# Last adaLN product moved from the attention steps to the output tiles, convolution projections spread over 22 steps

## The chip, the core and the metric

The kernel runs on one core of one Trainium2 chip. The metric is the device time of one execution in microseconds (us). TensorE (PE) does the matmuls, VectorE (DVE), ScalarE (ACT) and GpSimd (POOL) the rest, and SyncE (SP) issues most of the transfers. Each engine goes through its own list of instructions in order and waits on semaphores for the others.

## What is computed

One inference step of one decoder layer, for 512 prompt rows and 8 samples with a cache of 4096 rows each, all in float32. Cut to what matters here:

```python
sh1, sc1, ga1, sh2, sc2, ga2 = _adaln(c, w_ada, b_ada, 6)
h = _rms_norm(x, g_norm1) * (1.0 + sc1) + sh1
q, k, v, logf, conv_in, gate_b = _mixer_inputs(h, w_in, b_forget)   # gate_c * u, gate_b
attn = attend(q, k, v, logf)          # prompt: 512 rows; samples: 8 x 4096 cached rows
conv_y, new_buf = _short_conv(conv_in, conv_buf, conv_w)
x = x + ga1 * _merge_heads(attn, conv_y, gate_b, g_attn_out, g_conv_out, w_out)
h = _rms_norm(x, g_norm2) * (1.0 + sc2) + sh2
x = x + ga2 * _hier_moe(h, ...)       # 32 experts, 2 of them per row
...
shp, scp = _adaln(c_prompt, w_ada_final, b_ada_final, 2)
y_prompt = _rms_norm(xp, g_final) * (1.0 + scp) + shp
```

`_adaln(c, w, b, n)` is `silu(c) @ w + b`, cut into n parts. The product with `w_ada_final` (1024 x 2048, 8 MB) is used only at the very end, in the last norm. "The last adaLN product" is that one.

## The kernel before, in words

The order of all work is written out by hand, engine by engine. It has these parts:

- **Setup and projections** (to 187 us): the first adaLN product, the norm, and the projections for q, k and v. Every projection of the input is a "section" of 512 columns, loaded in two halves ("units" of 1 MB, u = 2 * section + half) into the three slots of region R_w. A slot is loaded again when its unit has been used.
- **The loop of 32 steps** (187 to 434 us), `for w in range(NT * H)`: step w is one head of one block of 128 prompt rows. On TensorE a step transposes the probabilities (`turn`, L644), in odd steps makes the scores of the next two heads (`score_pair`, L628 and L633), does some blocks of the convolution's three sections (`conv_block`, which calls L547; sections 3, 4 and 5 have 8 blocks each, and the table `CONV_IN_STEP` says which step does which), then one or two chunks of the samples' values (`values`, L512), then probabilities times v (`weigh`, L654). On VectorE a step takes one chunk of the samples' keys (`k_chunk`, L1503 and L1505), in odd steps the row maxima of the next two heads (`row_max`, L1671 and L1674), and the convolution's gates and taps. So `turn(w + 1)` can't begin before VectorE has passed `row_max(w + 1)`, which stands behind the key chunk of an odd step w.
- **The cache stream**: 64 key chunks and 64 value chunks of 1 MB each, alternating, gathered by GpSimd (L2121) into a ring of five slots in region R_kv. A chunk is asked for when the chunk five places before it has been used, and GpSimd waits for that in order.
- **The last adaLN product**, `late_ada(k)`, k = 0 to 7: 1 MB of `w_ada_final` and four matmuls (L385; each is two passes in the trace) into bank 1, in steps 19 to 26. SyncE loads the eight units (`late_load`, L2252) into the same three slots of R_w as units 12 to 19.
- **Output tiles** (from 434 us): `out_tile(t, after)` is eight parts of two matmuls with w_out (L802); behind the parts named in `after` stands one value chunk. Around them stand second norms, router (`route`, L877), and for the rest of the cache stream 11 key chunks and 22 value chunks.
- **Experts** (from 606 us): 32 experts with 3 MB of weights each, in five slots. Slot 0 is region R_q, where the loop has q, k and v.

SyncE's transfers go in order too: after the conv sections it issues the last adaLN units, some small vectors, w_out (into R_w once the last adaLN units have been used), and then, when the loop is over, the experts.

Of the kernel before, what the change touches and what calls it, by code (L numbers as in the profile page):

```python
# [44 lines left out]
SECS = 512  # L45


def build(nc, x_prompt, x_sample, c_prompt, c_sample, cache_k, cache_v, cache_logf, state_conv,
# [6 lines left out]
    with ctx:  # L55
# [81 lines left out]
        w_unit = view(R_w, 0, [3, 4, SECS])  # L137
        x_a = view(R_x, 0, [5, D])
# [183 lines left out]
        def step_values(w):  # L322
# [3 lines left out]
        CONV_IN_STEP = {0: (3, (0, 1)), 1: (3, (2,)), 2: (3, (3, 4)), 3: (3, (5,)), 4: (3, (6, 7)),  # L326
                        5: (4, (0,)), 6: (4, (1, 2)), 7: (4, (3,)), 8: (4, (4,)), 9: (4, (5,)), 10: (4, (6, 7)),
                        11: (5, (0,)), 12: (5, (1,)), 13: (5, (2,)), 14: (5, (3,)), 15: (5, (4,)), 16: (5, (5,)),
                        17: (5, (6,)), 18: (5, (7,))}
        SQUARE_AT = {14: 0, 16: 1, 18: 2, 20: 3, 21: 4}  # L330
# [44 lines left out]
        def _(pe):  # L375
# [365 lines left out]
            def spread_chunk(j):  # L741

                if j == 0:
                    pe.wait_ge(b_loaded[0], 32)
                out = take(0, ("mod_spread", j + 1) if j < 4 else ("mod_scaled", j - 3))
                spread_wide(j, out[:, :]).then_inc(S["expand_done"], 1)
# [11 lines left out]
            for w in range(NT * H):  # L758
# [48 lines left out]
            def out_tile(t, after):  # L807
                for half in range(2):
                    for k0 in range(0, KD, 2):
                        out_part(t, half, k0)  # L810
                        if 4 * half + k0 // 2 in after:
                            values(1)

            def sample_sums():

                pe.wait_ge(S["sum_ready"], B)
                for c in range(C4):
# [46 lines left out]
            def route(i):  # L864
# [4 lines left out]
                if i == 0:  # L869
                    pe.wait_ge(S["wr_loaded"], 64)  # L870
                    pe.wait_ge(S["part_ready"], 4)
# [179 lines left out]
        def _(act):  # L1051
# [52 lines left out]
            def ada_evac(g):  # L1104
                act.wait_ge(S["ada_done"], g + 1)
                copy(part[:, g - 1, :], bank[5 if g < 3 else 1][:, :]).then_inc(S["part_ready"], 1)
# [93 lines left out]
            def spread_evac(j):  # L1200
                act.wait_ge(S["expand_done"], j + 1)
                half = slice((j % 2) * SECS, (j % 2 + 1) * SECS)
                copy((ga1_p if j < 2 else sh2_p)[:, half], bank[0][:, :]).then_inc(S["mod_spread"], 1)
# [40 lines left out]
            for w in range(NT * H):  # L1244
# [22 lines left out]
                if w == 19:  # L1267
# [11 lines left out]
                if w == LAST_ADA_AT[-1] + 1:  # L1279
                    ada_evac(3)  # L1280
# [57 lines left out]
            sample_exp(7)  # L1338
            rows_turned(1)
# [90 lines left out]
        def _(dve):  # L1430
# [267 lines left out]
            def spread_scale(j):  # L1698
# [5 lines left out]
                V.scalar_tensor_tensor(sc2_p[:, lo], bank[0][:, :], 1.0, sc2_p[:, lo], ALU.add, ALU.mult)\  # L1704
# [10 lines left out]
            for w in range(NT * H):  # L1715
                if w in (7, 8, 10, 11):
                    gate_in({7: 0, 8: 1, 10: 2, 11: 3}[w])
                if w in (13, 15, 17, 19):
                    gate_out((w - 13) // 2)
                if w == 11:  # L1720
                    sample_gate_in()
                if w == 19:
                    sample_gate_out()
                if w in (27, 28):
                    spread_scale(w - 23)
# [9 lines left out]
                if 9 <= w < 13:  # L1735
                    taps(w - 9)
                if w == 12:
# [491 lines left out]
        def _(sp):  # L2229
# [17 lines left out]
            def late_load(k):  # L2247

                u = 12 + k
                name, count = unit_free["w", u - 3]  # L2250
                sp.wait_ge(S[name], count)
                sp.dma_start(w_unit[:, u % 3].rearrange("p j c -> p (j c)"), w_fin_v[:, k, :]).then_inc(unit_loaded[u % 3], 16)  # L2252
# [64 lines left out]
            for i in (2, 0, 1):  # L2317
                name, count = unit_free["w", 17 + (i + 1) % 3]
                sp.wait_ge(S[name], count)
                sp.dma_start(view(R_w, i * 2048, [2, D]), w_out_v[:, 2 * i:2 * i + 2, :]).then_inc(S["wo_loaded"], 16)  # L2320
            sp.wait_ge(S["part_ready"], 4)
            sp.dma_start(bias_rows(2), row(b_ada_final).rearrange("o (j c) -> (o j) c", c=SECS)).then_inc(b_loaded[1], 16)
# [21 lines left out]
            sp.wait_ge(S["outs"], 16 * 8)  # L2344
            sp.wait_ge(S["k_used"], NKV)
# [80 lines left out]
```

## Time and profile before

| | |
|---|---|
| median of three runs | 905.0 us (903.67 to 905.01) |
| profiled execution, its device time | 904.93 us |
| its span, first to last instruction | 903.1 us |
| TensorE busy | 754.0 us (83%) |
| VectorE busy | 532.7 us (59%) |
| moved by DMA | 311.80 MB, mean 345 GB/s |

The profiled execution is 0.07 us from the median, so sums can be made against it; 1.8 us of it lie outside the span. All times below count from the start of the span. No engine is busy throughout: the page gives shares over stages that have different limits, so each stage is read by itself.

### The profile page before, as it was taken

The page shows a single profiled execution, that of the slowest core. Times are in us where ns is not written, and L with a number is a line of the kernel's source. Part 1 is how long each engine was busy: PE and PEld are TensorE (multiplying, and loading weights), DVE is VectorE, ACT ScalarE, POOL GpSimd, SP SyncE. Part 2 cuts the span into 40 slices and gives each one's busy share as a digit, 9 for nine tenths or more (in the row PEclk, how much of TensorE's full clock was granted, in tenths as well). Part 3 has the DMA queues.
Part 4 walks back from the last instruction along what each step waited for, and adds up shares of the span by engine and source line. Part 5 has one row for each costly group of instructions (what it writes and reads, how often), then busy time and mean ns, then how long its engine had stood idle before and what let it go on. Part 6 is the DMA issues. An engine that isn't in the chain of part 4 may idle for free.

```text
span 903.1 us, 9755 instructions
## 1 busy us (share of the span) xinstructions
PE 754.0 (83%) x3872; PEld 356.9 (40%) x3872; DVE 532.7 (59%) x659; ACT 171.3 (19%) x359; POOL 269.6 (30%) x271
## 2 busy tenths in 40 slices
PE   4979999789999999889877797849999877878720
PEld 1623333234444333334322334425555544545500
DVE  3196896878499997598988812561333222222238
ACT  3200211021131233222301210322111101111102
POOL 2462124434235352523364310012232222222100
PEclk9889999999999995955899798758999999999965
DMA  8999599998997999999799984655999999999643
GB/s 346 397 409 407 208 347 364 416 418 335 353 327 293 374 379 419 408 362 419 307 365 369 375 338 186 256 196 195 411 408 411 410 409 411 410 409 406 254 154 148
DMA packets 67140, 311.80 MB, mean 345 GB/s; under 512 B 12195, under 2 KB 12687, under 8 KB 42006
## 3 DMA queue, kind: packets, MB, share of 16 engines
q1 hardware_dynamic: 39994, 161.11, 45.3%
q0 software_dynamic: 24496, 145.65, 41.0%
q10 hardware_dynamic: 2604, 4.40, 1.3%
q8 instruction: 31, 0.51, 0.2%
q14 instruction: 15, 0.12, 0.0%
HBM read 304.42 MB, written 14.98 MB: 354 GB/s over the span
## 4 chain that ended last, share of the span: by engine, by line
PE 38%; DMA 26%; DVE 20%; SPq 6%; issue 5%; ACT 2%; POOL 1%; POOLq 0%; DVEq 0%; ACTq 0%
PE bank L547 7%; DMA R_kv<-in_cache_k_dram,kv_index 6%; DVE R_kv L1503 6%; PE bank L965 6%; DMA R_kv<-in_w_expert_up_dram 5%; DVE R_sc L1505 4%; PE bank L512 4%; PE bank L989 3%; PE bank L802 3%; DMA R_w<-in_w_expert_up_dram 3%; DMA R_q<-in_w_expert_up_dram 3%; DMA R_cm<-in_w_expert_up_dram 3%; DMA R_kv<-in_cache_v_dram,kv_index 3%; DMA R_cm<-in_w_ada_dram 2%; SPq L2334 2%
## 5 line engine op out<-in xcount | busy, mean ns | idle before, releaser
L2121 POOL DMA_INDIRECT R_kv<-in_cache_k_dram,kv_index x64 | 99.0, 1546 | 164.6 <-DVE R_sc L1505 102.0
L1505 DVE TENSOR_REDUCE R_sc<-R_kv 128x32 f32<-128x2048 f32 x64 | 146.3, 2286 | 2.2
L547 PE MATMUL bank<-R_h,R_w 128*128 128x512 f32 x320 | 145.4, 604 | 0.0
L1503 DVE TENSOR_TENSOR R_kv<-R_kv,R_m 128x2048 f32<-128x2048 f32 x56 | 128.1, 2288 | 25.5 <-DMA R_kv<-in_cache_k_dram,kv_index 25.2
L2121 POOL DMA_INDIRECT R_kv<-in_cache_v_dram,kv_index x64 | 73.6, 1150 | 145.3 <-DVE R_sc L1505 79.6
L512 PE MATMUL bank<-R_kv,R_sc 128*8 128x512 f32 x512 | 76.1, 683 | 27.8 <-DMA R_kv<-in_cache_v_dram,kv_index 27.8
L547 PEld LDWEIGHTS bank<-R_h,R_w 128*128 128x128 f32 x320 | 59.4, 192 | 76.7 <-issue 75.6
L2183 POOL DMA_INDIRECT expert_rows_scratch<-R_h,R_m x32 | 32.2, 1007 | 188.9 <-DVE R_h L1979 188.9
L1970 DVE COPY R_h<-bank 128x128 f32<-128x128 f32 x32 | 9.3, 292 | 103.1 <-PE bank L981 103.1
L1974 DVE SCALAR_TENSOR_TENSOR R_h<-bank,R_m 128x512 f32<-128x512 f32 x32 | 24.0, 751 | 73.6 <-PE bank L989 73.6
L967 PE MATMUL bank<-R_kv,R_h 128*64 128x256 f32 x208 | 50.8, 401 | 0.0
L802 PE MATMUL bank<-R_w,R_cm 128*128 128x512 f32 x96 | 46.7, 626 | 1.0 <-issue 1.0
L1391 ACT ACTIVATE R_h<-bank 64x256 f32<-64x256 f32 x32 | 12.1, 377 | 186.3 <-PE bank L967 186.3
L2179 POOL DMA_INDIRECT R_t<-h_scratch,R_m x32 | 32.9, 1030 | 41.6 <-DVE R_m L1888 32.1
L512 PEld LDWEIGHTS bank<-R_kv,R_sc 128*8 128x8 f32 x512 | 8.9, 89 | 77.6 <-issue 38.8
L654 PEld LDWEIGHTS bank<-R_q,R_t 128*128 128x128 f32 x160 | 24.3, 224 | 33.4 <-issue 33.4
L1061 ACT ACTIVATE R_h<-bank 128x512 f32<-128x512 f32 (+1 forms) x41 | 24.5, 597 | 61.0 <-PE bank L974 46.6
L965 PE MATMUL bank<-R_kv,R_h 128*64 128x256 f32 x112 | 27.1, 398 | 7.1 <-DMA R_kv<-in_w_expert_up_dram 6.4
L965 PE MATMUL bank<-R_q,R_h 128*64 128x256 f32 x112 | 28.1, 408 | 5.5 <-DMA R_q<-in_w_expert_up_dram 4.7
L547 PE MATMUL bank<-R_w,R_h 128*128 128x512 f32 x64 | 30.9, 627 | 0.0
L965 PE MATMUL bank<-R_sc,R_h 128*64 128x256 f32 x96 | 23.5, 401 | 8.6 <-DMA R_kv<-in_w_expert_up_dram 8.6
L1061 ACT ACTIVATE R_t<-bank 128x512 f32<-128x512 f32 (+6 forms) x36 | 15.0, 420 | 79.4 <-PE bank L644 77.2
(371 smaller groups left out, 1225.3 us busy)
## 6 DMA issues: line engine op xcount, KB each, us to landing
R_cm<-in_w_ada_dram SPq DMA_DIRECT2D x19, 1024.0 KB, 9.3
R_kv<-in_w_expert_up_dram SPq DMA_DIRECT2D x13, 1024.0 KB, 23.2
R_kv<-in_w_expert_down_dram SPq DMA_DIRECT2D x13, 1024.0 KB, 22.4
R_w<-in_w_in_dram SPq DMA_DIRECT2D x12, 1024.0 KB, 11.8
R_w<-in_w_ada_final_dram SPq DMA_DIRECT2D x8, 1024.0 KB, 9.7
R_q<-in_w_expert_gate_dram SPq DMA_DIRECT2D x7, 1024.0 KB, 16.6
R_q<-in_w_expert_up_dram SPq DMA_DIRECT2D x7, 1024.0 KB, 22.7
R_q<-in_w_expert_down_dram SPq DMA_DIRECT2D x7, 1024.0 KB, 22.1
```

Of the source, the lines that this page charges most:

```text
L512: last = nc.tensor.matmul(out[32 * j:32 * j + H, :], scores[:, b, c * CH + j, :], kv_ring[ring_slot[g]][:, j, :], start=(c == 0), stop=(c ...
L547: last = nc.tensor.matmul(out, l, r, start=(k == 0), stop=(k == KD - 1))
L802: last = nc.tensor.matmul(bank[4 + 2 * (t % 2) + half][:, :], m, wo[k][:, half * 512:(half + 1) * 512], start=(k == 0), stop=(k == KD - 1))
L965: nc.tensor.matmul(bank[2 + xs][0:SLOTS, 0:DE], xe_t[xs][:, c, a, :], gw[:, a, c, :], start=(k == 0), stop=(k == 7))
L967: last = nc.tensor.matmul(bank[2 + xs][SLOTS:2 * SLOTS, 0:DE], xe_t[xs][:, c, a, :], uw[:, a, c, :], start=(k == 0), stop=(k == 7))
L989: last = nc.tensor.matmul(bank[4 + xs][half * SLOTS:(half + 1) * SLOTS, :], hid_t[xs][:, k, :], dw[:, k, half * 512:(half + 1) * 512], sta ...
L1061: return nc.scalar.activation(out, in_, ACT.Copy, scale=scale)
L1503: V.tensor_tensor(keys[:, :, :], keys[:, :, :], spread(q, [P, CH, HW]), ALU.mult).then_inc(S["k_products"], 1)
L1505: V.reduce_sum(scores[:, b, s * CH:(s + 1) * CH, :], keys.rearrange("p r (h d) -> p r h d", h=H), AX.X)\
L2121: pool.indirect_dma_start(kv_flat[ring_slot[g]][:, :], None, k_rows if kind == "k" else v_rows, bass.IndirectOffsetOnAxis(kv_index[:, n:n ...
L2179: return pool.indirect_dma_start(x_e[s][:, :], None, h2_dram, bass.IndirectOffsetOnAxis(col, 0), bounds_check=2 * (T + B) - 1, oob_is_err= ...
L2183: return pool.indirect_dma_start(y_dram, bass.IndirectOffsetOnAxis(col, 0), y_e[s][:, :], None, bounds_check=4 * (T + B) - 1, oob_is_err=F ...
```

## The change

The eight `late_ada` calls leave steps 19 to 26. Five stand now among the parts of the first two output tiles, one behind each named part, and three behind the value chunks and router that follow. Their weights go to the three slots of region R_q (`fin_unit`), which is free when the loop is over; SyncE issues them there, ahead of the experts, and expert 0 waits until the product is done. The product uses bank 0 instead of bank 1, and the spreading of the other adaLN parts bank 1 instead of bank 0. The 24 convolution blocks are spread over steps 0 to 21, nearly always one per step (before: 0 to 18, in six steps two or more), and everything behind them (gates, squares, spreads) moves three steps or so later.

```diff
+        fin_unit = view(R_q, 0, [3, 4, SECS])
...
-        CONV_IN_STEP = {0: (3, (0, 1)), 1: (3, (2,)), 2: (3, (3, 4)), 3: (3, (5,)), 4: (3, (6, 7)),
...
+        CONV_IN_STEP = {0: (3, (0, 1)), 1: (3, (2,)), 2: (3, (3,)), 3: (3, (4,)), 4: (3, (5,)), 5: (3, (6,)), 6: (3, (7,)),
...
-        SPREAD_AT = {20: 0, 21: 1, 22: 2, 23: 3, 26: 4, 27: 5}
-        LAST_ADA_AT = range(19, 27)
+        SPREAD_AT = {23: 0, 24: 1, 25: 2, 26: 3, 27: 4, 28: 5}
...
             def late_ada(k):
                 if k == 0:
-                    take(1, ("part_ready", 4))
+                    take(0, ("part_ready", 4))
                 u = 12 + k
                 pe.wait_ge(unit_loaded[u % 3], 16 * w_turn(u))
-                last = ada_block(w_unit[:, u % 3], k, bank[1])
+                last = ada_block(fin_unit[:, u % 3], k, bank[0])
...
-                if w == 19:
+                if w == 22:
                     conv_rows()
-                if w in LAST_ADA_AT:
-                    late_ada(w - LAST_ADA_AT[0])
...
-            out_tile(0, (1, 3, 5, 7))
-            out_tile(1, (1, 3, 5, 7))
+            out_tile(0, (1, 3, 5, 7), {4: 0, 6: 1})
+            out_tile(1, (1, 3, 5, 7), {0: 2, 4: 3, 6: 4})
             gather_values(5)
-            values(2)
+            values(1)
+            late_ada(5)
+            values(1)
             turn_rows(0)
+            late_ada(6)
             route(0)
-            values(2)
+            values(1)
+            late_ada(7)
+            values(1)
...
-            for k in range(3):
-                late_load(k)
-
             sp.wait_ge(S["acc_done"], 24)
             sp.wait_ge(S["samp_done"], 6)
-            for k in range(3, 8):
-                late_load(k)
...
             sp.wait_ge(S["pv_done"], NT * H)
             sp.wait_ge(S["outs"], 16 * 8)
+            for k in range(8):
+                late_load(k)
+            sp.wait_ge(S["part_ready"], 4)
+            sp.dma_start(bias_rows(2), row(b_ada_final).rearrange("o (j c) -> (o j) c", c=SECS)).then_inc(b_loaded[1], 16)
+            sp.wait_ge(S["ada_done"], 4)
             sp.wait_ge(S["k_used"], NKV)
             gate_up(0, 0)
```

How this moves instructions shows best in the order on TensorE. First step 2 of the loop (L644 is the turn at its head, L547 the convolution, four matmuls to a block, L512 a value chunk, L654 the weighing):

```order
 L654 MATMUL bank<-R_q,R_t 128x64
 L644 MATMUL bank<-ident,R_t 128x128
-L547 MATMUL bank<-R_h,R_w 128x512 x8
+L547 MATMUL bank<-R_h,R_w 128x512 x4
 L512 MATMUL bank<-R_kv,R_sc 8x512 x4
 L654 MATMUL bank<-R_q,R_t 128x64
```

One of the step's two blocks has gone to step 3; steps 4, 6 and 10 lose one in the same way, and three blocks of section 5 go beyond step 18. Then TensorE at steps 20 to 22, where the three blocks arrive (L385 is one unit of the last adaLN product, L732 a spread, L678 the samples' columns of the section just done):

```order
-L385 MATMUL bank<-R_w,c_t 32x512 x4
-L732 MATMUL bank<-R_p,selp 128x512
+L547 MATMUL bank<-R_h,R_w 128x512 x4
 L512 MATMUL bank<-R_kv,R_sc 8x512 x4
 L654 MATMUL bank<-R_q,R_t 128x64 x3
...
-L385 MATMUL bank<-R_w,c_t 32x512 x4
-L732 MATMUL bank<-R_p,selp 128x512
+L547 MATMUL bank<-R_h,R_w 128x512 x4
+L678 MATMUL bank<-sel,R_m 128x8 x4
 L512 MATMUL bank<-R_kv,R_sc 8x512 x4
```

A unit of the product and a spread have gone from each step, and a block of the convolution has come. Third, the second half of the first output tile in the change (L800 is the line of the output matmuls there, L385 now reads R_q):

```order
L800 MATMUL bank<-R_w,R_cm 128x512 x2
L385 MATMUL bank<-R_q,c_t 32x512 x4
L800 MATMUL bank<-R_w,R_cm 128x512 x2
L512 MATMUL bank<-R_kv,R_sc 8x512 x4
L800 MATMUL bank<-R_w,R_cm 128x512 x2
L385 MATMUL bank<-R_q,c_t 32x512 x4
L800 MATMUL bank<-R_cm 128x512 x2
L512 MATMUL bank<-R_kv,R_sc 8x512 x4
```

Before, the same place has only the output matmuls (L802) and the value chunks:

```order
L802 MATMUL bank<-R_w,R_cm 128x512 x4
L512 MATMUL bank<-R_kv,R_sc 8x512 x4
L802 MATMUL bank<-R_w,R_cm 128x512 x2
L802 MATMUL bank<-R_cm 128x512 x2
L512 MATMUL bank<-R_kv,R_sc 8x512 x4
```

So two value chunks have a unit of the product ahead of them there, and each unit waits for its own megabyte.

## Rows read from the trace of the kernel before

**Rows 1.** Stretches: PE, PEld, DVE, ACT, POOL busy us (x instructions), granted clock, DMA share, GB/s.

```profile
199.07:246.62 47.55, 47.36 (x205) 20.09 (x204) 31.85 (x30) 7.68 (x26) 16.41 (x14) 1.00 0.93 359
187.00:332.50 145.50, 142.70 (x631) 60.66 (x632) 122.34 (x134) 32.69 (x89) 58.70 (x57) 0.99 0.91 349
332.00:362.00 30.00, 27.05 (x119) 10.82 (x120) 22.79 (x22) 7.79 (x22) 7.85 (x7) 0.64 1.01 419
332.50:434.00 101.50, 92.26 (x432) 37.52 (x431) 81.03 (x76) 27.62 (x64) 34.47 (x29) 0.70 1.01 404
361.70:434.00 72.30, 66.01 (x320) 27.49 (x319) 58.53 (x55) 19.83 (x42) 26.92 (x22) 0.72 1.01 397
434.00:457.00 23.00, 17.46 (x77) 5.59 (x76) 20.85 (x24) 7.17 (x13) 8.13 (x8) 0.84 0.71 270
457.00:507.00 50.00, 36.79 (x140) 13.73 (x138) 42.12 (x29) 4.92 (x9) 25.52 (x19) 0.87 0.98 388
507.00:606.00 99.00, 79.80 (x393) 39.77 (x392) 46.26 (x125) 23.33 (x46) 7.95 (x16) 0.80 0.66 255
606.00:847.00 241.00, 209.04 (x1450) 126.84 (x1452) 64.71 (x117) 31.12 (x62) 62.10 (x61) 0.96 0.97 386
```

**Rows 2.** TensorE in order of time: step 2 and the head of step 3.

```profile
204.99 0.28 PE L644 MATMUL bank<-ident,R_t 128*128 128x128 f32 x1
205.11 7.03 PE L547 MATMUL bank<-R_h,R_w 128*128 128x512 f32 x16
213.32 0.28 PE L644 MATMUL bank<-ident,R_t 128*128 128x128 f32 x1
```

**Rows 3.** VectorE in order of time, step 7; in brackets idle before, and its releaser.

```profile
242.05 0.69 DVE L1607 TENSOR_TENSOR R_cm<-bank,R_cm 128x512 f32<-128x512 f32 x1 [6.86 <-PE bank L547]
```

**Rows 4.** TensorE: heads of steps 19, 20, 22, and instructions of steps 19 and 21.

```profile
332.54 0.50 PE L644 MATMUL bank<-ident,R_t 128*128 128x128 f32 x3
335.19 1.07 PE L385 MATMUL bank<-R_w,c_t 128*32 128x512 f32 x8
337.89 1.04 PE L512 MATMUL bank<-R_kv,R_sc 128*8 128x512 f32 x8 [1.63 <-DMA R_kv<-in_cache_v_dram,kv_index]
342.86 0.87 PE L644 MATMUL bank<-ident,R_t 128*128 128x128 f32 x3 [1.32 <-ACT R_cm L1061]
354.63 1.94 PE L385 MATMUL bank<-R_w,c_t 128*32 128x512 f32 x8
356.50 2.07 PE L732 MATMUL bank<-R_p,selp 32*128 32x512 f32 x2
361.66 0.85 PE L644 MATMUL bank<-ident,R_t 128*128 128x128 f32 x3
```

**Rows 5.** VectorE in order of time: the key chunk of step 25.

```profile
383.39 2.29 DVE L1503 TENSOR_TENSOR R_kv<-R_kv,R_m 128x2048 f32<-128x2048 f32 x1 [4.18 <-DMA R_kv<-in_cache_k_dram,kv_index]
```

**Rows 6.** SyncE: issues of the product's units 1 to 2 and 6 to 7; their landing.

```profile
323.75 6.74 SPq L2252 DMA_DIRECT2D R_w<-in_w_ada_final_dram  x2
364.43 6.62 SPq L2252 DMA_DIRECT2D R_w<-in_w_ada_final_dram  x2
DMA to landing us min/median/max: 8.7/9.7/9.9
```

**Rows 7.** The chain that ended last, first half of the loop: start, us, what.

```profile
222.99 7.64 DMA R_w<-in_w_in_dram
```

**Rows 8.** Groups by line, 434 to 507 us: busy, mean ns | idle before, releaser.

```profile
L1503 DVE TENSOR_TENSOR R_kv<-R_kv,R_m 128x2048 f32<-128x2048 f32 x11 | 25.2, 2289 | 7.4 <-DMA R_kv<-in_cache_k_dram,kv_index 7.3
L512 PE MATMUL bank<-R_kv,R_sc 128*8 128x512 f32 x96 | 15.5, 725 | 16.6 <-DMA R_kv<-in_cache_v_dram,kv_index 16.6
```

**Rows 9.** The chain that ended last, behind the second output tile.

```profile
490.90 9.89 DMA R_kv<-in_cache_v_dram,kv_index
502.73 1.82 PE bank L861 x8
505.71 1.98 PE bank L877 x16
```

More of the change, by code:

```diff
@@ L744, in spread_chunk @@
                     pe.wait_ge(b_loaded[0], 32)
-                out = take(0, ("mod_spread", j + 1) if j < 4 else ("mod_scaled", j - 3))
+                out = take(1, ("mod_spread", j + 1) if j < 4 else ("mod_scaled", j - 3))
                 spread_wide(j, out[:, :]).then_inc(S["expand_done"], 1)
@@ L805, in out_part, with out_tile @@
                     last.then_inc(S["wo_done"], 1)
-            def out_tile(t, after):
+            def out_tile(t, after, ada={}):
                 for half in range(2):
@@ L810, in out_tile @@
                         out_part(t, half, k0)
-                        if 4 * half + k0 // 2 in after:
+                        part_no = 4 * half + k0 // 2
+                        if part_no in after:
                             values(1)
+                        if part_no in ada:
+                            late_ada(ada[part_no])
             def sample_sums():
                 pe.wait_ge(S["sum_ready"], B)
+                pe.wait_ge(S["part_ready"], 4)
                 for c in range(C4):
@@ L1105, in ada_evac @@
                 act.wait_ge(S["ada_done"], g + 1)
-                copy(part[:, g - 1, :], bank[5 if g < 3 else 1][:, :]).then_inc(S["part_ready"], 1)
+                copy(part[:, g - 1, :], bank[5 if g < 3 else 0][:, :]).then_inc(S["part_ready"], 1)
             def sample_exp(b):
@@ L1202, in spread_evac @@
                 half = slice((j % 2) * SECS, (j % 2 + 1) * SECS)
-                copy((ga1_p if j < 2 else sh2_p)[:, half], bank[0][:, :]).then_inc(S["mod_spread"], 1)
+                copy((ga1_p if j < 2 else sh2_p)[:, half], bank[1][:, :]).then_inc(S["mod_spread"], 1)
             def spread_samples(half, done):
@@ L1338, in _ @@
             sample_exp(7)
+            ada_evac(3)
             rows_turned(1)
@@ L1703, in spread_scale @@
                 lo = slice((j % 2) * SECS, (j % 2 + 1) * SECS)
-                V.scalar_tensor_tensor(sc2_p[:, lo], bank[0][:, :], 1.0, sc2_p[:, lo], ALU.add, ALU.mult)\
+                V.scalar_tensor_tensor(sc2_p[:, lo], bank[1][:, :], 1.0, sc2_p[:, lo], ALU.add, ALU.mult)\
                     .then_inc(S["mod_scaled"], 1)
@@ L1715, in _ @@
             for w in range(NT * H):
[L1716 to L1720, printed above, removed]
+                if w in (9, 11, 13, 14):
+                    gate_in({9: 0, 11: 1, 13: 2, 14: 3}[w])
+                if w in (16, 18, 20, 22):
+                    gate_out((w - 16) // 2)
+                if w == 14:
                     sample_gate_in()
-                if w == 19:
+                if w == 22:
                     sample_gate_out()
-                if w in (27, 28):
-                    spread_scale(w - 23)
+                if w in (28, 29):
+                    spread_scale(w - 24)
                 if w in (29, 30, 31):
@@ L2316, in _ @@
                 sp.dma_start(wo[k], w_out_v[:, k, :]).then_inc(S["wo_loaded"], 16)
-            for i in (2, 0, 1):
-                name, count = unit_free["w", 17 + (i + 1) % 3]
+            for i in range(3):
+                name, count = unit_free["w", 9 + i]
                 sp.wait_ge(S[name], count)
                 sp.dma_start(view(R_w, i * 2048, [2, D]), w_out_v[:, 2 * i:2 * i + 2, :]).then_inc(S["wo_loaded"], 16)
-            sp.wait_ge(S["part_ready"], 4)
-            sp.dma_start(bias_rows(2), row(b_ada_final).rearrange("o (j c) -> (o j) c", c=SECS)).then_inc(b_loaded[1], 16)
             wg = w_expert_gate.rearrange("l e (a p c) f -> (l e) p a (c f)", a=2, c=4)
```

26 lines of the change are left out of this document (12 added, 14 removed).

## Prediction

> **What bounds the kernel now.** I read the page's slices first, cut the span into stretches where their pattern changes, and then looked in each stretch for the wait that ends last. Four stretches matter.
>
> Steps 0 to 18 (187 to 332.5 us): TensorE is busy 142.7 of 145.5 us at a clock of 0.99, VectorE only 122.3 [rows 1]. A step with two convolution blocks shows why: its two blocks are 7.03 of the 8.33 us from one turn to the next [rows 2], so a block is 3.5 us. VectorE has about 4.6 us of key chunk per step and then waits for TensorE, up to 6.86 us at a time [rows 3]. TensorE sets the pace, by the crowded steps. DMA moves 349 GB/s, below the 419 it shows at its fullest [rows 1].
>
> Steps 19 to 31 (332.5 to 434 us): here DMA moves 404 GB/s, in the first 30 us 419, and both other engines have gaps: TensorE waits for value chunks [rows 4], VectorE for key chunks, at worst 4.18 us [rows 5]. The product's units are in that stream: after the first one, seven of the eight are issued from 323.75 us to 371 us [rows 6]. TensorE also falls to half its clock (1.2 GHz instead of 2.4): a product takes 1.07 us in step 19 and 1.94 us in step 21, and the stretch's mean clock is 0.70 [rows 1, 4]. What the engine did just before the fall were two waits, 1.63 and 1.32 us [rows 4]. So this stretch is bound by DMA, and partly by a slow TensorE.
>
> Output tiles, 434 to 507 us: TensorE waits 16.6 us for value chunks, VectorE 7.3 us for key chunks [rows 8], and the chain goes through a value chunk that took 9.89 us to come [rows 9]. It is a DMA stretch with one gap: from 434 to 457 us only 270 GB/s, afterwards 388 [rows 1]. In the gap the ring is full and VectorE still finishes the loop.
>
> From 507 us on TensorE works through the remaining tiles (chunks and product have to be there by then); the experts after it take 241 us at 386 GB/s [rows 1], whenever they begin.
>
> **The change, part by part.**
>
> *Steps 0 to 18.* Three blocks leave: 3 x 3.5 = 10.5 us less of TensorE. The blocks that only change steps cost the same wherever they stand, as long as TensorE stays the bound, and it does: 142.7 - 10.5 = 132 us against VectorE's 122, of which two gates go to later steps too. Two waits come in. Section 5's second unit is loaded when block 6 of section 4 is done, which is now in step 13, and the samples' rows of section 5 need it in step 14. Behind it stand one block (3.5), the samples' columns (0.9), a value chunk (1.0), weighing, turn and half of the sample rows, about 7.3 us; a unit of w_in took 7.64 us when it was on the chain [rows 7]. Nothing to 3 us; I take 2, with everything later in the loop queued behind. And steps 1 to 6 become short: before 47.55 us, now three blocks and 2 us of sample rows less, 35 us, with 13 chunks and one unit of 1.05 MB each, 14.7 MB or 420 GB/s, where 359 were moved before [rows 1]. Some of it comes out of the ring's store; nothing to 6 us, I take 1.5. Sum: -10.5 + 2 + 1.5 = **-7**.
>
> *Steps 19 to 21.* Before 361.66 - 332.54 = 29.1 us. Of step 19 (10.3 us) 7 stay without product, turned rows and the wait of 1.63. Steps 20 and 21 (18.8 us) ran at half clock; without two products of 1.94 and two spreads of 2.07 they are 10.8, at full clock half of that [rows 4]: 12.5 us in all. Three blocks (10.5) and the samples' columns (0.9) come in. That is dense work, so I take the full clock: 24 us, **-5**. Nothing would be gained if it stayed at half clock.
>
> *Steps 22 to 31.* Before 72.3 us. VectorE was busy 58.5 us, TensorE 66.0 at mixed clocks, DMA moved 28.7 MB [rows 1]. VectorE gets a gate and the scaling with the spread, 60 us. TensorE loses five products and gets two spreads and the turned rows, some 3 us less. DMA loses some 2.5 MB of the product's units, 26.2 MB, at 404 GB/s 65 us. No engine needs more than 66 us, but they didn't overlap fully before either: 69 us, **-3.3**. The ends are 61 us (VectorE alone) and 80 us (TensorE at half clock through most of it: 62 us of work at a mean of 0.72 is 45 at full and 90 at half clock).
>
> *Output tiles to the first routed rows.* The 8.4 MB come in here. The stream in 73 us was 25.6 MB (23 x 270 and 50 x 388 GB/s); with the product 34.0 MB, which at 404 GB/s, what the loop's full stretch keeps up, are 84.2 us: **+11.2**. The first three units, issued when the loop ends, fall into the gap, which has 23 x (419 - 270) = 3.4 MB of room; the other five take turns with key and value chunks. From below: all the room of the stretch at 419 GB/s is used, 34.0 / 0.419 = 81 us, +8. From above: the chunks get half of the 419 GB/s for as long as the product's units flow, 8.4 MB / 0.21 = 40 us; in these they need 40 x 388 = 15.5 MB and get 8.4, which costs 7.1 MB or 17 us. TensorE's products themselves (six, 1.07 us each) hide in its 16.6 us of waits; with that cover gone they are 6 us.
>
> The row for how such a mixture flows is the first 30 us after step 19, where units of the product and chunks ran together: the sum was 419 GB/s, and units landed in 8.7 to 9.9 us [rows 1, 6], 106 to 120 GB/s for each. The Trainium skill ("DMA: Bandwidth & Descriptors", section "Issuing engines are not separate DMA queues") says that transfers issued by scalar, sync or gpsimd run on the same 16 engines and interleave. By it a load that is moved brings no bandwidth, which speaks against this change; the sum above goes the same way by its rows, and the strict half share is the rival below.
>
> *After that.* One product stands between two value chunks at 507 us, where the chain is on TensorE [rows 9]: **+1.1**. The one before it fits between the transposes and the router, where TensorE waits 1.2 us for ScalarE (504.55 to 505.71) [rows 9]. Expert 0's 3 MB, before issued with the last key chunk, now wait for the product; they have some 90 us, in which DMA moves 255 GB/s [rows 1]. Without that cover they would cost 8 us. The other small loads, gates and bank swaps move with the steps they belong to and are hidden by the same engines.
>
> Sum: -7 - 5 - 3.3 + 11.2 + 1.1 = -3.0. The profiled execution took 904.93 us, next to the median of 905.0, so **901.9 us**.
>
> **The rivals.** 0.2% (1.8 us) is about what a measurement of this kernel can tell from no change.
>
> 1. *Forecast: the loop wins some 15 us, the output tiles give back some 12.* 0.42, between 898 and 904.
> 2. *The tiles hide the loads.* If the loop ends nearer VectorE's bound (61 us for steps 22 to 31, -8 more) or the gap takes more than three units, the sum is 891 to 898. For it: 73 us of output tiles hold 5 MB of room at 419 GB/s. Against: the five later units can't be issued in the gap, since their slots are freed by products that stand in the tiles. 0.13.
> 3. *It cancels:* DMA is the bound from step 19 to 507 us in both, the bytes up to there are the same, and TensorE's gain in the first steps is only an earlier arrival at the same stream. For it: all but 40 us of the 320 us are needed at 419 GB/s (117.4 MB). Against: the short first steps use room that was idle (349 GB/s). 903 to 907, 0.21.
> 4. *Slower: the chunks are held to half* while the product's units flow, +17 instead of +11, and the products, each in front of a value chunk, wait for their own unit; a late value chunk holds its ring slot, GpSimd's queue and so the next key chunk. 907 to 910. It decides when the first routed rows come more than 88 us after the loop's end. For it: five slots only, and 16.6 us of waits already. Against: the 419 GB/s of mixed traffic. 0.17.
> 5. *Slower: half clock* in most of steps 22 to 31, 80 us instead of 69: 913. For it: the convolution, which kept TensorE busy, is not there, and the clock was 0.72 in these steps. Against: they were so before too, with less of a gap in between. 0.07.
>
> The range reaches into 2, 4 and 5: **892 to 911**. Faster by over 0.2%, under 903.2: all of 2 and 0.38 of 1, 0.51. Within: the rest of 1 and 0.19 of 3, 0.23. Slower: 4, 5 and the rest of 3, 0.26.
>
> **What would show it.** Step 19 should begin some 138 us after step 0 (before 145.3, from rows 1 and 4), with no step of over 10 us but 0, 13 and perhaps 19; step 22 some 162 us after it; the loop's end at 231 us (before 247). In steps 19 to 21 the blocks should take 3.5 us each, and VectorE's waits for keys be nearly gone. From the loop's end to the router of the first rows some 84 us instead of 72, at over 400 GB/s, with no hole behind the loop. From there to the end the same time as before within 2 us. The forecast is wrong if the loop shortens by less than 10 us, if a product in the tiles waits for its unit by several us, or if key chunks wait over 15 us in sum in the tiles.

## The result, and the profile after

The changed kernel takes 920.4 us, median of four runs (915.7 to 923.9), against 905.0 for the kernel before: ratio 1.014, interval 1.010 to 1.019. Taken again later, beside 25 runs of the kernel before with a median of 907.6, it took 920.6, ratio 1.014 (1.007 to 1.020). The forecast was 901.9 in a range of 892 to 911, so it was wrong, in sign too. Executions more than 1.5% above the fastest of their kernel are left out of the medians and ratios in this document: 2 of 31 and 1 of 23 of the kernel before, 5 of 10 without the product's loads, 2 of 10 with the table alone, 3 of 12 with three units in the loop. The ratios stand as recorded, with their 95% intervals, and differ a little from the quotients of the two medians. The profiled execution of the changed kernel took 923.87 us, its span is 922.1. Its stretches, in the columns of [rows 1], cut where step 0, 19 and 22 begin, where the loop ends, and at the router of the first rows:

```profile
189.16:341.61 152.45, 139.53 (x599) 57.09 (x600) 121.55 (x131) 31.67 (x85) 59.85 (x57) 0.92 0.84 321
341.61:365.69 24.08, 22.76 (x113) 11.14 (x113) 20.33 (x24) 6.52 (x19) 10.75 (x7) 1.00 0.91 349
365.69:443.24 77.55, 71.25 (x290) 31.09 (x289) 61.60 (x56) 21.46 (x46) 28.04 (x23) 0.63 0.88 333
443.24:524.06 80.82, 61.23 (x259) 18.66 (x257) 62.26 (x52) 12.09 (x22) 32.21 (x26) 0.87 1.01 415
524.06:922.10 398.04, 304.82 (x1952) 174.99 (x1948) 140.09 (x281) 63.40 (x126) 73.02 (x80) 0.89 0.81 318
```

Steps 0 to 18 were to shrink from 145.3 to 138 us and have grown to 152.5. The first row shows that this is no longer TensorE's work: it is busy 139.5 of 152.5 us, at a clock of 0.92 where [rows 1] have 0.99. Steps 19 to 21 came out as forecast (24.1 us at full clock), steps 22 to 31 did not (77.6 us against a forecast of 69, at a clock of 0.63). The output tiles take 80.8 us at 415 GB/s (forecast 84), what follows 398.0 (before 397.4).

Two steps hold the loss of the first stretch. TensorE in order of time, steps 7 and 14:

```profile
236.22 0.28 PE L644 MATMUL bank<-ident,R_t 128*128 128x128 f32 x1
237.69 1.07 PE L464 MATMUL bank<-R_w,R_h 128*32 128x512 f32 x8
241.07 1.93 PE L464 MATMUL bank<-R_w,R_h 128*32 128x512 f32 x8 [2.32 <-DMA R_w<-in_w_in_dram]
242.94 5.85 PE L547 MATMUL bank<-R_h,R_w 128*128 128x512 f32 x8
249.96 0.28 PE L644 MATMUL bank<-ident,R_t 128*128 128x128 f32 x1
...
296.50 0.39 PE L644 MATMUL bank<-ident,R_t 128*128 128x128 f32 x2
296.82 1.07 PE L464 MATMUL bank<-R_w,R_h 128*32 128x512 f32 x8
305.96 1.93 PE L464 MATMUL bank<-R_w,R_h 128*32 128x512 f32 x8 [8.07 <-DMA R_w<-in_w_in_dram]
307.82 5.83 PE L547 MATMUL bank<-R_h,R_w 128*128 128x512 f32 x8
315.06 0.39 PE L644 MATMUL bank<-ident,R_t 128*128 128x128 f32 x2
```

L464 is the samples' rows of a new section, one group of matmuls for each half. In step 7 the second half (unit 9) has to be waited for, in step 14 again (unit 11). The wait is only part of the price: behind it TensorE runs at half clock (granted clock 0.61 from 240.0 to 248.8 us, 0.60 from 305.96 to 313.65). Eight such matmuls take 1.93 instead of 1.07 us, the block behind them 5.85 and 5.83 instead of 3.70. Step 7 takes 13.7 us and step 14 18.6. The chain that ended last goes through both loads (start, us, what):

```profile
227.63 13.40 DMA R_w<-in_w_in_dram
290.91 15.01 DMA R_w<-in_w_in_dram
```

They took 13.4 and 15.0 us. For the second the prediction had reckoned with 7.64 [rows 7]; the first it had not looked at. GpSimd, which asks for the cache chunks, shows why the second took so long:

```profile
275.11 0.94 POOL L2126 DMA_INDIRECT R_kv<-in_cache_k_dram,kv_index  x1 [4.56 <-DVE R_sc L1510]
276.41 5.74 POOL L2156 TENSOR_SCALAR_AFFINE_SELECT later<-later 128x64 f32<-128x64 f32 x8 [0.15 <-POOL later L2153]
282.60 0.94 POOL L2126 DMA_INDIRECT R_kv<-in_cache_v_dram,kv_index  x1 [0.44 <-issue]
283.84 0.94 POOL L2126 DMA_INDIRECT R_kv<-in_cache_k_dram,kv_index  x1 [0.30 <-issue]
285.08 1.96 POOL L2126 DMA_INDIRECT R_kv<-in_cache_v_dram,kv_index  x1 [0.31 <-issue]
287.35 0.94 POOL L2126 DMA_INDIRECT R_kv<-in_cache_k_dram,kv_index  x1 [0.30 <-issue]
288.82 0.94 POOL L2126 DMA_INDIRECT R_kv<-in_cache_v_dram,kv_index  x1 [0.54 <-DVE R_sc L1510]
```

Behind key chunk 34 GpSimd builds a small table (`halves`, the 64-column selects). For 5.74 us it asks for nothing, and nothing is left in flight (4 and 0 GB/s from 280 to 284 us). Then it asks for five chunks in 6.2 us. Unit 11 is issued 2 us after the last of them. From its issue to its landing, 290.91 to 305.92 us, the DMA queues moved (packets, MB, share of the 16 engines; q0 holds GpSimd's gathers, q1 SyncE's loads):

```profile
q0 software_dynamic: 681, 4.94, 80.2%
q1 hardware_dynamic: 528, 1.05, 18.3%
```

So the unit shared 400 GB/s with 4.94 MB of chunks: the 2.9 MB that were left of the five, of which 2.3 MB had moved by then, and 2.0 MB of the two that GpSimd asked for at 296.4 and 300.3 us, while the unit was still under way. Its last 0.02 MB came after 302 us, beside 1.44 MB of chunks. (The expectations below count the five chunks and the unit instead, 6.3 MB or 15.2 us. That comes close by chance: part of the burst had moved before the unit was issued, and later chunks took its place.) In the kernel before, unit 11 was issued at 269.0 and the table began at 282.6, so the burst, four chunks there, came behind it:

```profile
269.02 0.37 SPq L2238 DMA_DIRECT2D R_w<-in_w_in_dram  x1
...
282.57 5.74 POOL L2151 TENSOR_SCALAR_AFFINE_SELECT later<-later 128x64 f32<-128x64 f32 x8
```

The change has moved the load from ahead of the pause to behind it.

### The profile page after: what moved, and what is told of

Read it like the earlier page. It is cut to its first block, busy times and chain, and to the rows that moved or that the text cites. A ratio compares the mean times of both kernels' runs of the same rounds, so it can differ in the third digit from the quotient of the medians.

```text
span 922.1 us, 9757 instructions
## 1 busy us (share of the span) xinstructions
PE 756.9 (82%) x3872; PEld 355.7 (39%) x3872; DVE 533.2 (58%) x659; ACT 171.2 (19%) x359; POOL 270.0 (29%) x271
## 4 chain that ended last, share of the span: by engine, by line
PE 46%; DMA 26%; DVE 15%; SPq 5%; issue 4%; ACT 2%; POOL 1%; ACTq 0%; POOLq 0%; DVEq 0%
PE bank L547 11%; PE bank L971 6%; DMA R_kv<-in_cache_v_dram,kv_index 6%; DMA R_kv<-in_w_expert_up_dram 5%; PE bank L512 5%; DVE R_kv L1508 4%; PE bank L800 4%; PE bank L995 4%; DVE R_sc L1510 3%; DMA R_w<-in_w_in_dram 3%; DMA R_w<-in_w_expert_up_dram 3%; DMA R_q<-in_w_expert_up_dram 3%; DMA R_cm<-in_w_ada_dram 3%; DMA R_cm<-in_w_expert_up_dram 3%; PE bank L654 2%
## 5 line engine op out<-in xcount | busy, mean ns | idle before, releaser
L547 PE MATMUL bank<-R_h,R_w 128*128 128x512 f32 x320 | 150.9, 621 | 0.0
L2126 POOL DMA_INDIRECT R_kv<-in_cache_k_dram,kv_index x64 | 92.7, 1448 | 194.4 <-DVE R_sc L1510 100.8
L2126 POOL DMA_INDIRECT R_kv<-in_cache_v_dram,kv_index x64 | 78.6, 1228 | 135.3 <-DVE R_sc L1510 69.8
L512 PE MATMUL bank<-R_kv,R_sc 128*8 128x512 f32 x512 | 77.0, 687 | 30.4 <-DMA R_kv<-in_cache_v_dram,kv_index 30.3
L547 PEld LDWEIGHTS bank<-R_h,R_w 128*128 128x128 f32 x320 | 60.9, 198 | 81.3 <-issue 80.1
L973 PE MATMUL bank<-R_kv,R_h 128*64 128x256 f32 x208 | 49.2, 391 | 0.0
L800 PE MATMUL bank<-R_w,R_cm 128*128 128x512 f32 x96 | 48.8, 643 | 0.0
L512 PEld LDWEIGHTS bank<-R_kv,R_sc 128*8 128x8 f32 x512 | 8.8, 89 | 77.5 <-issue 39.8
L654 PEld LDWEIGHTS bank<-R_q,R_t 128*128 128x128 f32 x160 | 24.9, 230 | 33.4 <-issue 32.5
L971 PE MATMUL bank<-R_kv,R_h 128*64 128x256 f32 x112 | 25.5, 380 | 7.0 <-DMA R_kv<-in_w_expert_up_dram 6.4
L547 PE MATMUL bank<-R_w,R_h 128*128 128x512 f32 x64 | 30.9, 627 | 0.0
```

What stands on the lines that cost most here:

```text
L512: last = nc.tensor.matmul(out[32 * j:32 * j + H, :], scores[:, b, c * CH + j, :], kv_ring[ring_slot[g]][:, j, :], start=(c == 0), stop=(c ...
L547: last = nc.tensor.matmul(out, l, r, start=(k == 0), stop=(k == KD - 1))
L654: last = nc.tensor.matmul(bank[5][:, h * HD:(h + 1) * HD], probs_t[w % 2][:, b, :], v_r[:, b, h * HD:(h + 1) * HD], start=(b == 0), stop=( ...
L800: last = nc.tensor.matmul(bank[4 + 2 * (t % 2) + half][:, :], m, wo[k][:, half * 512:(half + 1) * 512], start=(k == 0), stop=(k == KD - 1))
L971: nc.tensor.matmul(bank[2 + xs][0:SLOTS, 0:DE], xe_t[xs][:, c, a, :], gw[:, a, c, :], start=(k == 0), stop=(k == 7))
L973: last = nc.tensor.matmul(bank[2 + xs][SLOTS:2 * SLOTS, 0:DE], xe_t[xs][:, c, a, :], uw[:, a, c, :], start=(k == 0), stop=(k == 7))
```

## The experiments

The theories, by the letters that the expectations use. A: late units of w_in lengthen the loop, and with them in time the forecast holds. B: something else takes over the wait. C: the 8.4 MB of the product in the output tiles are the cost. D: the w_out loads, all issued at step 22 now, starve the cache stream. E: the clock falls in steps 22 to 31 anyway. F: unit 11 is late because of GpSimd's burst. G: every load beside the cache stream is that slow. H: half clock holds up steps 22 to 31. I: there, more work only costs more. All ran beside runs of the kernel before on the same chip, whose medians were 907.7, 907.6 and 906.9 in the three groups (901 to 917 in all, so one profile alone says little about a total). Steps ahead of the first wait repeat within a few hundredths of a us, steps behind waits by several: in the two profiles of the changed kernel steps 0 to 18 took 152.5 and 149.6 us, steps 22 to 31 77.6 and 83.1.

**Units asked for earlier.** Block 6 of sections 3 and 4, after which the next section's second unit can be loaded, one step earlier:

```diff
-   ... 4: (3, (5,)), 5: (3, (6,)), 6: (3, (7,)), ... 12: (4, (5,)), 13: (4, (6, 7)),
+   ... 4: (3, (5, 6)),              6: (3, (7,)), ... 12: (4, (5, 6)), 13: (4, (7,)),
```

> The change as it is, but block 6 of section 3 one step earlier (step 4 instead of 5) and block 6 of section 4 one step earlier (12 instead of 13), so that the slots for units 9 and 11 come free a step earlier. Theory A (two late units of w_in lengthen the loop): steps 7 and 14 fall from 13.7 and 18.6 us to about 8.5 and 9 us, the loop from 254 to about 240 us, total 904 to 908 us. Theory B (something else holds the loop, the cache stream or VectorE, and takes over the wait): steps 7 and 14 get shorter and others longer, total 915 us or more.

912.3 us, ratio 1.004 (0.9995 to 1.008). Step 7 is cured: 8.2 us, no wait. Step 14 is not: 16.6 us, for the unit, issued 8.4 us earlier by the count from step 0, now falls into the middle of the burst and takes 18.3 us. So the lead was not the cause there.

**The product alone.** The change without the spreading: convolution, gates, squares and spreads at the steps of the kernel before, the product in the tiles.

> Only the product is moved to the output tiles; the convolution stays in steps 0 to 18 as before, spreads in steps 20 to 27 (on the other bank). Theory A (the spreading made the units late, the product's move is nearly neutral): steps 0 to 18 as before, 145 us; steps 19 to 31 without the product's units 88 to 95 us instead of 101; tiles to the first router 81 us instead of 72; total 902 to 908 us. Theory C (the product's 8.4 MB in the tiles are what costs): total 915 us or more.

907.8 us, ratio 1.001 (0.996 to 1.005). In its profile the loop is 240.8 us (before 246.9) and the tiles 78.3 (before 71.6): what the steps win, the tiles give back.

**No loads of the product.** 1 KB of each unit instead of 1 MB:

```diff
-   sp.dma_start(fin_unit[:, u % 3].rearrange("p j c -> p (j c)"), w_fin_v[:, k, :])
+   sp.dma_start(fin_unit[0:16, u % 3, 0, 0:16], w_fin_v[0:16, k, 0:16])
```

> The change, but of each megabyte of w_ada_final only 1 KB is loaded (the product then works on what lies in the region, so the last adaLN part is not computed). Theory A: the loop keeps its 254 us, the tiles to the first router fall from 81 to about 72 us, total 910 to 912 us, still slower than before. Theory C: total at or under 905 us.

908.2 us, ratio 1.001 (0.995 to 1.007); all ten executions lie between 902.0 and 923.2. The tiles take 69.0 us instead of 80.8, so the loads cost 11.8 us there. Yet the kernel is still no faster than before: steps 0 to 18 are as long as in the changed kernel (150.8 us). C is a part, not the whole.

**w_out one load at a time.** The first experiment, with each of the three w_out loads held for one more spread (`sp.wait_ge(S["mod_spread"], 2 + i)`).

> As e1_units_early, and in addition the three 1 MB loads of w_out wait for the second, third and fourth spread, so they are issued one by one in steps 24 to 27 instead of all at once at step 22. Theory D (the burst of 4.2 MB at step 22 starves the cache stream, TensorE and VectorE idle there and TensorE stays at half clock): steps 22 to 31 fall from 77 to about 70 us, total 5 to 8 us under e1_units_early. Theory E (the clock falls there anyway, since these steps give TensorE too little to do): steps 22 to 31 stay at 75 us or more, total within 2 us of e1_units_early.

915.2 us, ratio 1.006 (1.001 to 1.010), beside 912.3 without it: no gain. Steps 22 to 31 took 75.2 us at a clock of 0.66, beside 78.0 at 0.65 without it, where D wanted about 70. So D falls as the main cause.

**No burst.** The first experiment, and the table built behind key chunk 15, ahead of the loop, where GpSimd waits anyway:

```diff
-                if (kind, n) == ("k", 34):
+                if (kind, n) == ("k", 15):
```

> The block order of e1_units_early, and the small table that GpSimd builds behind key chunk 34 (5.74 us on its queue, then five cache chunks asked for in a row) built behind key chunk 15, ahead of the loop. Theory F: unit 11 took 15.0 us because it was asked for right behind that burst: six MB at some 413 GB/s are 15.2 us. Then the unit lands in 7 to 9 us here, step 14 takes 7 to 9 us instead of 16.6, steps 0 to 18 together 137 to 139 us as I had predicted, and the loop is about 8 us shorter than in e1_units_early (242 us). The time falls by about as much only if nothing gives it back: 904 to 908 us. Rival G: every load that comes beside the cache stream takes 13 to 18 us here, burst or not: then step 14 stays over 13 us.

905.8 us, ratio 0.998 (0.995 to 1.002); the profiled execution was the fastest of the ten (898.8 us, its span 897.1). Unit 11 lands in 8.2 us, beside 2.0 MB of chunks, and nothing waits for it: in step 14 both halves run in one group, and step 14 takes 7.3 us.

```profile
287.69 0.39 PE L644 MATMUL bank<-ident,R_t 128*128 128x128 f32 x2
288.01 1.92 PE L464 MATMUL bank<-R_w,R_h 128*32 128x512 f32 x16
289.86 3.70 PE L547 MATMUL bank<-R_h,R_w 128*128 128x512 f32 x8
294.96 0.39 PE L644 MATMUL bank<-ident,R_t 128*128 128x128 f32 x2
```

Its stretches, cut at the same places as above:

```profile
184.65:322.37 137.72, 132.97 (x599) 55.71 (x600) 121.61 (x131) 31.57 (x85) 56.44 (x48) 0.98 0.93 357
322.37:346.45 24.08, 22.76 (x114) 11.13 (x113) 20.34 (x24) 6.52 (x19) 10.75 (x7) 1.00 0.92 355
346.45:418.01 71.56, 58.86 (x290) 26.48 (x289) 61.27 (x56) 21.24 (x46) 25.84 (x23) 0.76 0.92 350
418.01:499.17 81.16, 61.93 (x259) 19.12 (x257) 61.78 (x51) 12.08 (x22) 30.36 (x26) 0.85 1.01 416
499.17:897.10 397.93, 304.89 (x1952) 175.21 (x1948) 140.42 (x281) 63.43 (x126) 73.07 (x80) 0.89 0.81 320
```

Steps 0 to 18 take 137.7 us (forecast 138), step 22 begins 161.8 us after step 0 (forecast 162). In the four profiles of kernels with both the earlier units and the moved table, steps 0 to 18 take 137.7 to 139.2 us. F holds, with the count of bytes as given above. G falls for step 14, but unit 10 shows what was right in it: in this same execution it took 16.0 us, beside 5.6 MB of GpSimd's transfers, nearly all of them chunks, at 417 GB/s in sum, with no table near. Nothing waits for it, since it is used only in step 14.

**The table alone.** The changed kernel with only the table moved.

> The changed kernel with only the small table built ahead of the loop. Theory F: step 7 stays at 13 to 14 us (its units came late for another reason), step 14 falls from 18.6 to under 10 us; 911 to 916 us where the changed kernel takes 920. Rival G: both steps as in the changed kernel.

909.9 us, ratio 1.003 (0.999 to 1.007), a little under the 911 to 916 expected. Step 14 takes 8.8 us, with a wait of 1.3 us left, and unit 11 lands in 8.3 us. Step 7 stays long, 15.5 us where 13 to 14 were expected; its unit is late for the other reason. In the profiles step 14 takes 7.3 to 9.3 us in all five kernels that spread the blocks and have the table moved, and 13.5 to 19.8 in the six executions of those that have it behind key chunk 34.

**Denser work in steps 22 to 30.** The no-burst kernel, with work for TensorE whose result is written over:

```diff
+                if 22 <= w < 31:
+                    for k in range(8):
+                        nc.tensor.matmul(bank[4][:, k % 4 * P:(k % 4 + 1) * P], ident[:], block64[:], start=True, stop=True)
```

> e5_units_early_no_burst with eight idle matmuls of 128x128 by 128x128 more on TensorE ahead of the turn of each step from 22 to 30 (into columns that the turn writes over; 1.8 us a step at full clock). Theory H: the half clock (mean 0.63 to 0.66 in steps 22 to 31) is what holds these steps at 75 to 78 us: with denser work the clock stays higher and the steps take no longer in spite of 16 us more work, perhaps 70 us. Rival I: the clock stays at half, the work of 16 to 32 us lies on the path, and the steps take 90 us or more. If VectorE or the chunks were the bound, the added work would be hidden and the steps stay at 75 to 78 us with the clock as it was.

903.4 us, ratio 0.998 (0.995 to 1.001). Steps 22 to 31:

```profile
352.00:422.08 70.08, 64.24 (x418) 39.12 (x416) 59.87 (x55) 21.25 (x46) 24.93 (x22) 0.93 0.93 356
```

The first of the nine groups of added matmuls stands ahead of the turn of step 22, so its 1.8 us count to step 21 here and in the two experiments below. From step 19 to the loop's end it is 96.0 us, beside 95.7 without the added work. So that work cost nothing and brought back the clock, but won nothing over a clock of 0.76: in the no-burst kernel VectorE, busy 61 of the 71.6 us and waiting for key chunks for 9.4, sets the pace of these steps.

**The changed kernel again**, beside these three.

> The changed kernel unaltered, beside the same runs of the kernel before as the others: 915 to 924 us as in its first four runs, ratio 1.01 to 1.02.

920.6 us, ratio 1.014 (1.007 to 1.020). Steps 7 and 14 took 11.6 and 19.8 us, steps 22 to 31 83.1 us at a clock of 0.59.

**The kernel before without the burst.** Its table behind key chunk 15.

> The kernel before with only GpSimd's small table built behind key chunk 15 instead of 34: does the gain of e5_units_early_no_burst come from the change or from the table? In the kernel before the burst came behind the loading of unit 11 and no engine waited for it, so by theory F nothing changes: 902 to 908 us, ratio 0.997 to 1.003. If the pause in the cache stream itself cost time, it is faster by 2 to 7 us like the others.

905.6 us, ratio 0.999 (0.997 to 1.002): nothing, as expected. The pause is harmless where no load waits behind it.

**Denser work in the changed kernel alone.**

> The changed kernel with only the eight idle matmuls in each step from 22 to 30. Theory H: in the changed kernel steps 22 to 31 are long (77.4 and 83.2 us in two profiles, at a mean clock of 0.63 and 0.59; 71.5 at 0.76) because of the half clock: with the filling the clock is over 0.85 there, the steps take 71 to 74 us, steps 7 and 14 stay as long as they are, and the whole takes 909 to 915 us instead of 920. Rival: the steps are long because the waits ahead of them left the cache stream in another phase; then they stay over 76 us at the higher clock.

914.9 us, ratio 1.013 (1.008 to 1.018). The median is 5 us below the changed kernel's, but the intervals overlap, so the total doesn't settle it; the profile does for the steps. Steps 22 to 31:

```profile
358.10:429.40 71.30, 64.25 (x418) 38.74 (x415) 59.53 (x55) 21.27 (x46) 24.75 (x22) 0.93 0.90 347
```

71.3 us, with more work, against 77.6 and 83.1 without it; from step 19 to the loop's end 98.8 us, against 101.6 and 108.9. So in these profiles H holds for the changed kernel, where the clock was 0.63 and 0.59, by less than the first figures say. Steps 7 and 14, which stand ahead of the added work, took 9.4 and 14.2 us in this execution (13.7 and 18.6, 11.6 and 19.8 without it), not what they took before as expected: the length of such a wait changes by some us from one execution to the next, another reason not to put the total down to the clock.

**Three units of the product back in the loop.** The no-burst kernel with the first three units in the slots of R_w that sections 4 and 5 leave, multiplied in steps 22 and 23, the sum put back into the bank in the tiles; spreads two steps later:

```diff
+        FIRST_ADA_AT = {22: (0, 1), 23: (2,)}
...
+                if k == 3:
+                    pe.wait_ge(S["part_ready"], 4)
+                    out = take(0, ("part_ready", 5))
+                    nc.tensor.matmul(out[:, :], ident[:], part[:, 2, :], start=True, stop=False)
...
-            out_tile(0, (1, 3, 5, 7), {4: 0, 6: 1})
-            out_tile(1, (1, 3, 5, 7), {0: 2, 4: 3, 6: 4})
+            out_tile(0, (1, 3, 5, 7))
+            out_tile(1, (1, 3, 5, 7), {0: 3, 4: 4})
...
+            for k in range(3):
+                late_load(k)
             sp.wait_ge(S["acc_done"], 24)
```

> e5_units_early_no_burst with three of the eight units of the product loaded and multiplied in steps 22 and 23 again (into the slots that section 4 and 5 leave), their sum kept in SBUF and put back into the bank by one matmul with the identity; the spreads two steps later; five units stay in the output tiles. If the output tiles are bound by bytes (81.2 us at 416 GB/s), 3.1 MB less are 7.5 us less there: 74 us; steps 22 to 31 have room (350 GB/s in 71.6 us) and grow by 0 to 3 us. 898 to 903 us, ratio 0.990 to 0.996. If the tiles are bound by something else, they stay at 80 us and nothing is won.

898.2 us, ratio 0.990 (0.986 to 0.993): faster than both kernels. Steps 22 to 31, then the output tiles:

```profile
349.02:426.37 77.35, 69.96 (x314) 30.95 (x312) 61.92 (x56) 21.95 (x47) 28.50 (x23) 0.67 0.91 347
426.37:499.13 72.76, 57.09 (x237) 18.41 (x235) 60.41 (x51) 12.08 (x22) 32.73 (x24) 0.84 1.01 413
```

The tiles lose 8.4 us (81.2 to 72.8) for 3.1 MB, as bytes at 413 GB/s would have it (7.6). Steps 22 to 31 take 77.4 us, 5.8 more where 0 to 3 were expected, at a clock of 0.67. So these two profiles show a gain of only 2.6 us over the no-burst kernel, whose profile is of its fastest execution; the rest of the difference in the ratios (0.990 to 0.998) they don't place.

**The same with the denser work.**

> e11_three_units_in_loop with the idle matmuls of e7_dense_filling as well: 0 to 4 us below e11 if the half clock still costs something there, the same if not.

895.5 us, ratio 0.987 (0.982 to 0.992). In its profile steps 22 to 31 are at full clock and shorter by 9.6 us:

```profile
354.03:421.82 67.79, 62.88 (x442) 37.70 (x439) 59.46 (x55) 21.74 (x47) 27.87 (x22) 0.97 1.01 395
```

Steps 19 to 21 took 3.5 us longer in that execution, 1.8 of them for the first group of added matmuls; from step 19 to the loop's end it is 95.4 us, beside 101.5. That the total is below the kernel without the filling isn't settled, since the intervals overlap; that it is below the kernel before is.

## Why the prediction was wrong, by its own steps

The forecast was -3.0 us, the spans of the two profiles differ by +19.0. Of the 22 us between, 14 lie in steps 0 to 18 and 8.4 in steps 22 to 31; the other parts differ by 2 us or less each.

*Steps 0 to 18: here it failed.* Of its three terms the -10.5 for the blocks was right: L547 is busy 86.6 us there in the kernel before and 77.8 in the no-burst kernel, 1.7 of these through half clock in step 12. The "nothing to 3 us; I take 2" for unit 11 was not: TensorE waited 8.07 us for it, and step 14 took 18.6 us where it takes 7.3 without the wait. The 1.5 us for the chunks of the short steps 1 to 6 were not needed there (35.0 us, as reckoned without them), but the denser stream of these steps met unit 9, and step 7 took 13.7 us where 8.2 are enough. With both waits gone the stretch is 137.7 us against the 138 forecast; with them it is 152.5 and 149.6 in the two profiles, so the waits and what came behind them cost 12 to 15 us. The medians of the two kernels are 14.8 us apart (905.8 and 920.6), though these differ in steps 22 to 31 too. Three things were missed.

First, the landing of 7.64 us [rows 7] was one row of one moment, used for another: it is unit 9 in the kernel before, with 1.4 MB of chunks beside it. The lead of 7.3 us was right (7 us passed from the issue of unit 11 to its need), the load took 15.0. The prediction's own [rows 6], with 8.7 to 9.9 us, give 1.4 to 2.6 us of waiting, no more than it took; for the 15 us one had to ask what else would be in flight at the new moment. The table stood in the trace of before, at 282.57 us, 6 us behind the use of unit 11 (the row above).

Second, the wait was priced without its tail. [Rows 4] had already shown half clock behind a wait: the granted clock of the kernel before is 1.00 from 338.86 to 340.45 us and 0.50 from there to 342.86. So the fall came behind the 1.63 us and ahead of the 1.32, not behind both as the prediction has it. Behind the 8.07 us the rows and block took about 3 us longer. Third, step 7 wasn't looked at: unit 9 landed in 13.4 us, with 4.1 MB of chunks beside it, where it took 7.64 before with 1.4 MB. The wait is cured by an earlier issue; that the denser stream is its cause was not tested by itself.

The experiments with a wait removed one at a time show each: with the table moved, step 14 falls from 18.6 to 8.8 us; with the earlier units, step 7 from 13.7 to 8.2; with both, the stretch takes what was forecast. That it then meets 138 so closely is luck in part. The forecast holds 3.5 us for the waits above, and none of them is left. In their place TensorE waits 3.17 us for ScalarE at the end of step 11 (1.32 in the kernel before), and two blocks behind that take 8.73 us where [rows 2] have 7.03:

```profile
268.95 0.41 PE L644 MATMUL bank<-ident,R_t 128*128 128x128 f32 x2 [3.17 <-ACT R_cm L1067]
269.19 8.73 PE L547 MATMUL bank<-R_h,R_w 128*128 128x512 f32 x16
```

*Steps 19 to 21: right.* 24.1 us for 24, at full clock, in this profile, in the no-burst kernel and with three units in the loop; 25.7 or 25.8 in five others with the same steps, 25.9 to 27.6 in the three with 1.8 us of added matmuls in them.

*Steps 22 to 31: too low, and rival 5 came in part.* Forecast 69 us, at least 70.1 measured with the full product in the tiles, without added work 71.5, since VectorE is busy 61 us there and waits for keys besides (9.4 us in the no-burst kernel); the changed kernel's 77.6 and 83.1 are above. The half clock is the reason as far as the one profile with the added work shows (71.3 us at 0.93), as rival 5 said with 80 us. The chance given to it, 0.07, was low. The prediction's argument against it (less of a gap between) was wrong: in step 24 of the changed kernel VectorE and TensorE both wait for a chunk, and what follows on TensorE is at half clock (a weighing takes 1.97 us, at full clock 1.10):

```profile
381.40 2.29 DVE L1508 TENSOR_TENSOR R_kv<-R_kv,R_m 128x2048 f32<-128x2048 f32 x1 [6.20 <-DMA R_kv<-in_cache_k_dram,kv_index]
```
```profile
385.18 1.90 PE L512 MATMUL bank<-R_kv,R_sc 128*8 128x512 f32 x8 [4.04 <-DMA R_kv<-in_cache_v_dram,kv_index]
387.00 1.97 PE L654 MATMUL bank<-R_q,R_t 128*128 128x64 f32 x8
```

Why the mean clock of these steps is 0.75 or 0.76 in three kernels of the change and 0.59 to 0.69 in five others with nearly the same work stays open.

*Output tiles: right in kind and nearly in size.* +9.2 us (80.8 against 71.6), forecast +11.2, between the bounds of 8 and 17; the stream runs at 415 GB/s, no product waits for its unit, and the first routed rows come 80.8 us after the loop, below the 88 us from which rival 4 would have decided. VectorE's key waits there sum to 15.9 us, a little over the 15 that the prediction named as a sign of being wrong. That the bytes are the price is shown from both sides: without the loads 69.0 us, with five eighths of them 72.8 and 73.7, and with all of them 78.3 to 81.2 in nine profiles.

*After that: right.* 398.0 us against 397.4, forecast +1.1; expert 0, issued at 536.9 us behind the product, costs nothing that shows.

With the failed step mended, the sum by the no-burst profile is -7.6 (steps 0 to 18), -5.0, -0.9, +9.6 and +0.5: -3.4 where the forecast had -3.0. That profile is of the fastest of ten executions, and its step 0 begins 2.6 us earlier besides, which the sum leaves out. The measured difference of medians is -1.8 us, with an interval (-4.9 to +1.4) that holds both that and nothing. So even then the change is close to rival 3: it takes 13.5 us from the loop and gives 9.6 back in the tiles. What wins is what rival 3 points at, loading where the stream has room: eight units in the tiles fill them, and with three of the eight ahead of them the whole is faster, though steps 22 to 31 then grow by 5.8 us.

The Trainium skill ("DMA: Bandwidth & Descriptors", "Issuing engines are not separate DMA queues") says that transfers issued by different engines interleave on the same 16 engines. The trace agrees and adds the price for a single load of 1.05 MB: 8.2 us where GpSimd moved 2.0 MB beside it (unit 11, no burst), 15.0 where it moved 4.9 (unit 11, changed kernel), 16.0 where it moved 5.6 (unit 10, no burst). In the prediction it was weighed for the tiles, where it was right, and not for the loop, where it decided.

## What to carry to other kernels

When a load's issue moves, ask what is in flight at the new moment, and read every queue that feeds the same DMA engines there; a load's duration from another moment is not its duration. A pause on a queue that refills a ring ended in a burst here, and the load issued behind it shared the engines with what was left of the burst and with the chunks asked for next. Price a wait of TensorE with the slow matmuls behind it, and move bytes only into stretches whose rate shows room.

## What the runs showed that I had not expected

A TensorE that is busy 71.3 of 77.6 us still had a mean granted clock of 0.63. Behind the wait of 4.04 us in step 24 it stayed at half clock for 50 us in which it was busy 48.5 (columns of [rows 1]):

```profile
385.18:435.03 49.85, 48.53 (x164) 20.93 (x164) 40.34 (x43) 14.51 (x31) 15.00 (x14) 0.50 0.85 328
```

Eight added 128x128 matmuls in each of nine steps, their result written over, brought the mean to 0.93, and from step 19 to the loop's end it took 2.8 and 10.1 us less than in the two profiles without them, the added work included.

Executions of the kernel before spread from 902.0 to 917.5 us on one chip, while the steps ahead of a wait repeat within a few hundredths (step 1: 5.92 and 5.93 us in all profiles).
